# Adding gate sums and causal mask to attention scores: products on TensorE, or VectorE on PSUM

## The reference, cut to what matters

```python
log_f = jax.nn.log_sigmoid(f_logit).transpose(0, 2, 1)       # head x token
cum = jnp.cumsum(log_f, axis=-1)
for blk in range(n_blocks):                                  # 2 blocks of 128 queries
    logits = jnp.einsum('bhqd,bhkd->bhqk', qb, kb).astype(jnp.float32) * scale
    logits = logits + cum[:, :, start:end, None] - cum[:, :, None, :end]
    mask = jnp.arange(end)[None, :] <= (start + jnp.arange(Q_BLOCK))[:, None]
    logits = jnp.where(mask, logits, -jnp.inf)
    p = jax.nn.softmax(logits, axis=-1)
    outs.append(jnp.einsum('bhqk,bhkd->bhqd', p.astype(v.dtype), vb))
```

## Time and profile before

| What | Value |
|---|---|
| median of three runs | 3310.09 us |
| profiled execution, first to last instruction (span) | 3309.2 us |
| PE busy | 3296.3 us, 100% |
| PE weight loads busy | 2762.8 us, 83% |
| DVE busy | 2270.2 us, 69% |
| ACT busy | 1578.3 us, 48% |
| POOL busy | 731.1 us, 22% |
| DMA, mean | 243 GB/s |

### The profile page before, as it was taken

One profiled execution on the slowest core, in us unless ns is written; L12 is line 12 of the kernel. 1 busy time (PEld: TensorE's weight loads), 2 busy tenths in 40 slices (PEclk: granted clock), 3 DMA queues, 4 the chain that ended last, 5 costly groups with the idle time before them and its releaser, 6 DMA issues.

```text
span 3309.2 us, 42798 instructions
## 1 busy us (share of the span) xinstructions
PE 3296.3 (100%) x15846; PEld 2762.8 (83%) x15846; DVE 2270.2 (69%) x2218; ACT 1578.3 (48%) x1289; POOL 731.1 (22%) x559
## 2 busy tenths in 40 slices
PE   9999999999999999999999999999999999999999
PEld 7888888888888888878888888888888888888887
DVE  6675545698888788866577497444444777777778
ACT  7344344443333333354465345777777433333433
POOL 0000002400000000121000188888883000000000
PEclk9999999999999999999999999999999999999999
DMA  7555556888888888867555556777777666666663
GB/s 280 192 193 192 186 194 235 314 310 334 320 311 318 315 305 314 306 246 293 215 191 202 181 206 216 216 212 214 208 216 242 235 236 246 246 232 239 243 234 133
DMA packets 159559, 803.95 MB, mean 243 GB/s; under 512 B 51668, under 2 KB 52484, under 8 KB 70496
## 3 DMA queue, kind: packets, MB, share of 16 engines
q1 hardware_dynamic: 85728, 610.05, 50.2%
q0 software_dynamic: 67248, 170.03, 16.2%
q10 hardware_dynamic: 6480, 22.44, 1.8%
HBM read 759.23 MB, written 43.18 MB: 242 GB/s over the span
## 4 chain that ended last, share of the span: by engine, by line
PE 97%; ACT 1%; DMA 1%; DVE 0%; issue 0%; POOL 0%; SPq 0%; ACTq 0%
PE ps L2243 24%; PE ps L2245 24%; PE ps L2244 24%; PE ps L2763 12%; PE ps L2772 6%; PE ps L2283 1%; PE ps L2320 1%; PE ps L2322 1%; PE ps L2321 1%; DMA raw<-in_w_first 1%; PE ps L2431 0%; PE ps L2411 0%; ACT hi L648 0%; PE ps L2820 0%; PE ps L2419 0%
## 5 line engine op out<-in xcount | busy, mean ns | idle before, releaser
L648 ACT CAST hi<-raw 128x2048 fp32r<-128x2048 f32 x571 | 1090.9, 1912 | 1526.6 <-PE ps L2245 1354.8
L1279 DVE TENSOR_TENSOR lo<-raw,hi 128x2048 fp32r<-128x2048 f32 x436 | 997.6, 2290 | 364.6 <-ACT hi L648 349.0
L2243 PE MATMUL ps<-hi,hT 128*128 128x512 f32 x2064 | 816.0, 395 | 0.0
L2245 PE MATMUL ps<-hi,hT 128*128 128x512 f32 x2064 | 804.4, 390 | 0.0
L2244 PE MATMUL ps<-lo,hT 128*128 128x512 f32 x2064 | 803.9, 389 | 0.0
L2243 PEld LDWEIGHTS ps<-hi,hT 128*128 128x128 f32 x2064 | 387.7, 188 | 82.3 <-issue 4.8
L2245 PEld LDWEIGHTS ps<-hi,hT 128*128 128x128 f32 x2064 | 387.5, 188 | 82.1
L2244 PEld LDWEIGHTS ps<-lo,hT 128*128 128x128 f32 x2064 | 387.9, 188 | 77.6
L588 POOL DMA_INDIRECT w_scratch<-picks,cell x256 | 397.7, 1553 | 86.3 <-issue 83.8
L2763 PE MATMUL ps<-hT,hi 128*128 128x512 f32 x1728 | 412.2, 391 | 0.0
L2243 PE MATMUL ps<-hi,pactTh 128*128 128x512 f32 x992 | 386.6, 390 | 0.0
(11 more groups left out here) (424 smaller groups left out, 3111.2 us busy)
## 6 DMA issues: line engine op xcount, KB each, us to landing
raw<-in_w_peer SPq DMA_DIRECT2D x256, 1024.0 KB, 5.0
raw<-in_w_ffn SPq DMA_DIRECT2D x132, 1024.0 KB, 5.9
adaraw<-in_w_ada POOLq DMA_DIRECT2D x96, 1024.0 KB, 5.2
raw<-in_w_first SPq DMA_DIRECT2D x86, 1024.0 KB, 4.9
raw<-in_w_second SPq DMA_DIRECT2D x72, 1024.0 KB, 4.9
raw<-in_w_merge SPq DMA_DIRECT2D x28, 1024.0 KB, 6.0
w_scratch<-zeros POOLq DMA_DIRECT2D x16, 1024.0 KB, 11.8
wc<-w_scratch POOLq DMA_DIRECT2D x32, 512.0 KB, 4.8
```

The lines of the kernel that those rows point to most:

```text
L648: nc.scalar.copy(hi[:, s, :], raw[:, s, :]).then_inc(hi_done, 1)
L1279: V.tensor_tensor(lo[:, s, :], raw[:, s, :], hi[:, s, :].bitcast(F32), ALU.subtract).then_inc(lo_done, 1)
L2243: T.matmul(out, th[stat], hi[:, s, cut], start=start, stop=False)
L2245: return T.matmul(out, tl[stat], hi[:, s, cut], start=False, stop=stop)
```

## The change: what it does

The products with `gates` and with the causal mask are gone, and so are `lsums`, `gates`, the rounded identity and mask. The sums go once to DRAM (`cum_d`, with their negatives), and come back in two forms: `cumrow`, for each head its negative sums as a row on all 128 partitions, and `cumq`, for each head the sum at the query as a column. POOL adds the mask to a copy of the first half of the rows (`cumdiag`) and to the second half in place. DVE then adds column and rows to the scores in PSUM, one instruction for each block of queries, before it takes the maxima.

```diff
-            nc.gpsimd.memset(gates[:].bitcast(F32), 0.0).then_inc(sem("sel_in"), 1)
+            nc.gpsimd.memset(zeros[:], 0.0).then_inc(sem("sel_in"), 1)
             pool.wait_ge(sem("sel_in"), 2)
-            nc.gpsimd.memset(gates[0:4].bitcast(F32), 1.0).then_inc(sem("sel_in"), 1)
-            nc.gpsimd.memset(zeros[:], 0.0).then_inc(sem("sel_in"), 1)
...
             clear_weights(0, 6)
-            pool.wait_ge(sem("cum"), 2)
-            load_sums(0)
-            clear_weights(6, 13)
-            pool.wait_ge(sem("scores2"), 4)
-            load_sums(1)
-            clear_weights(13, 16)
+            pool.wait_ge(sem("cum"), 1)
+            pool.dma_start(cum_d, lgate[:, 1:3, :]).then_inc(sem("cum_in"), 16)
+            pool.wait_ge(sem("cum_in"), 16)
+            pool.dma_start(cumrow[:], bass.AP(cum_d.tensor, SEQ, [[0, P], [2 * SEQ, H2], [1, SEQ]])).then_inc(sem("cum_in"), 16)
+            with nc.allow_non_contiguous_dma(reason="a column of sums for each head"):
+                for k in range(TOK):
+                    pool.dma_start(cumq[:, k], bass.AP(cum_d.tensor, P * k, [[1, P], [2 * SEQ, H2]])).then_inc(sem("cum_in"), 16)
+            pool.wait_ge(sem("cum_in"), 64)
+            later = causal[:].rearrange("p (o n) -> p o n", o=1).to_broadcast([P, H2, P])
+            nc.gpsimd.tensor_tensor(cumdiag[:], cumrow[:, :, 0:P], later, ALU.add).then_inc(sem("sel_in"), 1)
+            nc.gpsimd.tensor_tensor(cumrow[:, :, P:SEQ], cumrow[:, :, P:SEQ], later, ALU.add).then_inc(sem("sel_in"), 1)
+            clear_weights(6, 16)
...
-                S = [lsums[:, r, :] for r in range(4)]
-                step(V.tensor_copy(S[0], L[1]))
-                step(V.tensor_tensor(S[1], L[1], S[0].bitcast(F32), ALU.subtract))
-                V.tensor_scalar(S[2], S[0].bitcast(F32), -1.0, None, ALU.mult).then_inc(sem("cum"), 1)
-                V.tensor_scalar(S[3], S[1].bitcast(F32), -1.0, None, ALU.mult).then_inc(sem("cum"), 1)
+                V.tensor_scalar(L[2], L[1], -1.0, None, ALU.mult).then_inc(sem("cum"), 1)
...
                         dve.wait_ge(sem("scores2"), h + 1)
+                        dve.wait_ge(sem("sel_in"), 4)
+                        for k, sums in enumerate((cumdiag, cumrow)):
+                            part = ps[:, 6, SEQ * k:SEQ * k + P * (k + 1)]
+                            ins = V.scalar_tensor_tensor(part, part, cumq[:, k, h:h + 1], sums[:, h], ALU.add, ALU.add)
+                        step(ins)
...
-                        V.tensor_copy(identr[:], ident[:]).then_inc(sem("wfl"), 1)
-                        V.tensor_copy(causalr[:], causal[:]).then_inc(sem("wfl"), 1)
...
-                    pe.wait_ge(sem("pair_in"), 64)
-                    pe.wait_ge(sem("wfl"), 3)
...
-                    T.matmul(out, qkT2[:, h, P * m:P * m + P], qkT2[:, 8 + h, 0:keys], start=True, stop=False)
-                    T.matmul(out, gates[:, 0, h % 4, P * m:P * m + P], gates[:, 1, h % 4, 0:keys], start=False, stop=False)
-                    ins = T.matmul(ps[:, 6, SEQ * m + P * m:SEQ * m + keys], identr[:], causalr[:], start=False, stop=True)
+                    ins = T.matmul(out, qkT2[:, h, P * m:P * m + P], qkT2[:, 8 + h, 0:keys], start=True, stop=True)
```

More of the change, by code:

```diff
@@ L144 @@
     "gy_T": "ACT: gelu of the turned gates", "qk_T": "DVE: turned queries and keys out of PSUM",
-    "wf_in": "DMA: forget weights", "wfh": "ACT: their leading part", "wfl": "DVE: and rest; then identity and causal mask rounded", "f_mm": "PE: forget logits",
+    "wf_in": "DMA: forget weights", "wfh": "ACT: their leading part", "wfl": "DVE: and rest", "f_mm": "PE: forget logits",
     "lg_abs": "DVE: logits' size, then -|lambda|", "lg_exp": "ACT: their exponentials", "cum": "DVE: sums of log gates",
-    "sel_in": "Pool: zeros around the forget weights, zeros, then ones around the log gates' sums, a row of zeros", "pair_in": "DMA: sums of four heads as rows", "scores2": "PE: heads' scores", "max2": "DVE: maxima",
+    "sel_in": "Pool: zeros around the forget weights, a row of zeros, log gates' sums with the causal mask",
+    "cum_in": "DMA: log gates' sums in DRAM, then as rows and as columns", "scores2": "PE: heads' scores", "max2": "DVE: maxima",
     "exp2": "ACT: exponentials (two a head)", "turned2": "PE: turned probabilities", "probs2": "DVE: these out of PSUM",
@@ L247, in program @@
     bx = at("bx", [P, 8, SEQ], F32, XO + 8 * K)
-    gates = at("gates", [P, 2, 4, SEQ], F32R, XO)
+    cumrow = at("cumrow", [P, H2, SEQ], F32, XO)
+    cumdiag = at("cumdiag", [P, H2, P], F32, XO + 8 * K)
     probs2 = at("probs2", [P, 2, TOK, SEQ], F32, A + 41 * K)
@@ L255, in program @@
     lgate = at("lgate", [8, 4, SEQ], F32, A + 49 * K)
-    lsums = at("lsums", [8, 4, SEQ], F32R, A + 49 * K)
     ga1 = at("ga1", [P, D], F32, A + 24 * K)
@@ L276, in program @@
     cell = at("cell", [P, TOK, 8, TOPK], U32, A + 51 * K)
-    zeros = at("zeros", [P, 2048], F32, XO + 8 * K)
+    zeros = at("zeros", [P, 1024], F32, XO + 12 * K)
     y = at("y", [P, TOK, D], F32, A)
@@ L295, in program @@
     causal = at("causal", [P, P], F32, CO + 4 * K)
-    identr = at("identr", [P, P], F32R, CO + 3 * K)
-    causalr = at("causalr", [P, P], F32R, CO + 3 * K + 512)
     small_at = [CO + 5 * K + 512]
@@ L324, in program @@
     row0 = at("row0", [P, 1], F32, CO + 4 * K + 256)
+    cumq = cmb[:].rearrange("p e k g -> p (e k g)")[:, 0:TOK * H2].rearrange("p (k h) -> p k h", h=H2)
     ps = nc.alloc_psum_tensor("ps", [P, 8, 512], F32)
@@ L358, in program @@
     w_d = nc.dram_tensor("w_scratch", [EXPERTS, SEQ], F32, kind="Internal").ap()
+    cum_d = nc.dram_tensor("sums_scratch", [H2, 2, SEQ], F32, kind="Internal").ap()
     hid_d = nc.dram_tensor("hidden_scratch", [EARLY - 1, P, TOK * 512], F32, kind="Internal").ap()
@@ L540, in _ @@
             pool.wait_ge(sem("x_moved"), 32)
-            nc.gpsimd.memset(gates[:].bitcast(F32), 0.0).then_inc(sem("sel_in"), 1)
+            nc.gpsimd.memset(zeros[:], 0.0).then_inc(sem("sel_in"), 1)
             pool.wait_ge(sem("sel_in"), 2)
-            nc.gpsimd.memset(gates[0:4].bitcast(F32), 1.0).then_inc(sem("sel_in"), 1)
-            pool.wait_ge(sem("sel_in"), 3)
-            nc.gpsimd.memset(zeros[:], 0.0).then_inc(sem("sel_in"), 1)
-            pool.wait_ge(sem("sel_in"), 4)
             def clear_weights(first, last):
@@ L551, in clear_weights @@
                     part = w_d[1024 * i:1024 * i + 1024].rearrange("(r a) t -> r (a t)", a=8)
[L552 to L556, removed]
+                    row = zeros[:].rearrange("p (o n) -> p o n", o=1).to_broadcast([P, 2, 1024])
+                    pool.dma_start(part.rearrange("r (o n) -> r o n", o=2), row).then_inc(sem("w_zero"), 16)
             clear_weights(0, 6)
-            pool.wait_ge(sem("cum"), 2)
-            load_sums(0)
-            clear_weights(6, 13)
-            pool.wait_ge(sem("scores2"), 4)
-            load_sums(1)
-            clear_weights(13, 16)
+            pool.wait_ge(sem("cum"), 1)
[10 more added lines that the diff above has]
+            clear_weights(6, 16)
             pool.wait_ge(sem("values2"), H2)
@@ L2631, in scores2 @@
                     pe.wait_ge(sem("qk_T"), 4)
-                    pe.wait_ge(sem("pair_in"), 128)
                 for m in range(TOK):
```

## The result

Five runs of the changed kernel took 3322.64 to 3324.12 us, median 3323.07; the kernel before, beside them, 3309.64 to 3311.64, median 3310.09. The ratio is 1.0039, 95% interval 1.0028 to 1.0049: slower by 13.0 us, and clear of noise. The forecast was 3319.8, the range 3312.5 to 3326.0. The profiled run was the longest of the five, 3324.12, with a span of 3322.5 us.

The account below looks back on a forecast made before the run. PE, busy for 112.81 of 113.00 us in the second attention, was taken as the bound. Head 0's late sums 6.0, clock 2.0 and heads 1 to 7 1.65 made +9.7: 3319.8 us, range 3312.5 to 3326.

Parts of the forecast that it names:

- dearer sums: Rival: at head 0 columns take 10.3, weight pieces and rows sharing engines; +9.7 there, 3323.5 us in all; chance 0.14.
- PE bounds, and its idle time is not taken back: Second attention: PE busy 112.81 of 113.00 us, so any wait moves the end by as much.
- g = 0.44 a head: PE's scores: four products of 0.11 us go at each head, 3.5 us for eight if PE never waited.
- d = 0.77 a head: DVE ahead of the maxima: two additions on PSUM and a wait add 0.77 us, bounds 0.52 and 1.00.
- d - 0.33 net where the pattern is bare: Heads 1, 4, 5 and 6: the turning starts 0.44 us later each, +1.76 together.
- Head 0: +6.0: Head 0's turning: sums return late through DRAM and POOL, so PE turns at 1540.0 instead of 1533.99.
- lands, with 6.6, at 1532.7: Sums' return for head 0: last columns issued at 1526.1 land after 6.6 us; bounds 1529.0 and 1536.4.
- The clock: +2.0, 0 to 3: Behind head 0's 6.2 us of PE idleness the clock falls to half and costs 2.0 us.
- The rival of prompt sums: Columns land after 2.9, head 0 costs +2.3, PE idles 2.5 us, clock holds: +4.0, 3314.1 us; chance 0.20.
- What costs nothing: DVE's dropped casts and small instructions, POOL's dropped fills, and ten clearing DMAs now behind the additions: no cost.

Follow-up runs that it names:

- e6: Changed kernel with sums fetched early from an input tensor, and DVE's additions and maxima moved ahead of the next `lo`: 3306.90 us.
- e2: Changed kernel with rows and columns fetched from an input tensor before the first clearing, so not the gate's sums: 3311.85 us.
- e3: Changed kernel without the two DMAs of columns; DVE adds 0.0 in the same instruction: 3320.21 us.
- e4: Changed kernel with the rows fetched early from an input tensor and only the columns late: 3318.47 us.
- e5: Changed kernel with a partition's rows laid out in DRAM as one run of 8 KB instead of eight of 1 KB: 3321.24 us.
- e9: The changed kernel run once more, unedited, beside e10: 3322.36 us.
- e11: Changed kernel with no columns and a partition's rows as one run of 8 KB: 3317.79 us.
- e10: e1 run once more, beside the changed kernel: 3323.33 us.
- e12: e2 with a third addition on 128x256 a head on DVE ahead of the maxima: 3315.77 us.
- e1: Changed kernel with 38 products of ones by ones put on PE ahead of head 0's turning, to fill its idle time: 3322.05 us.

## Why the prediction was right

It forecast a slowdown of 9.7 us; 13.0 came, inside the range. Each link of its path is in the trace, but the time came out 0.4 us below that of its rival "dearer sums", and the range held because it was drawn wide enough for that case. By its own steps:

1. *PE bounds, and its idle time is not taken back.* Right: behind the turning of head 7 the two traces run on 13.0 to 13.3 apart to the end.
2. *g = 0.44 a head.* Right in size: 0.46 to 0.48 in e6. That it would not be gained was right too (e2), and that it would be there once DVE's way is shorter was shown by e6.
3. *d = 0.77 a head, d - 0.33 net where the pattern is bare.* d was 0.78. The net was 0.47, 0.31 and 0.30 at heads 4, 5 and 6 for a forecast of 0.44; head 3 had 0.73 for 0.77, heads 2 and 7 -0.58 and -0.52 for -0.44. All in all heads 2 to 7 cost 0.71 where my terms give 1.21. A part is how it is read: a load that had waited starts with its product, one in the flow 0.2 ahead of it. The rest is not accounted for.
4. *Head 0: +6.0.* The mechanism was right, the size was off: 9.46 less 0.28, so 9.2. The step that failed is "lands, with 6.6, at 1532.7". The last columns landed at about 1536.2, after 10.3. I had counted the megabyte of rows ahead of them with its 0.9 of issue and no time of its own; e3, e4 and e5 show that it is the rows. That was the rival "dearer sums", forecast at 3323.5 with 0.14; its reason, weight pieces and rows that share the engines, is shown for the rows and argued for the pieces. The other links were near: DRAM 1.8 for 2.5, POOL 2.33 for 2.40 each, POOL's end to the turning 2.5 for 2.43.
5. *The clock: +2.0, 0 to 3.* Right in size: 2.6 in the changed kernel's trace, 1.4 in that of e9. It fell about 4.5 us after the last product's end at 1534.19 (0.87 is the mean of the window from 1538), at the program's end 4.9. In e3, e4, e5 and e11 it was 4.7 to 5.2, but in e9 2.1. So 4.9 was no bound to lean on. The rival of prompt sums took it for granted that the clock holds through 2.5 us of idleness; it fell behind 2.3 us in e10 and behind 1.9 in e12.
6. *What costs nothing.* Right: in this stretch no wait of PE for `lo`, for a weight piece or for the clearings shows in the changed kernel's trace.

Sum with the measured terms: 9.2 + 0.3 + 2.6 + 0.3 (head 1) + 0.7 = 13.1, against 13.3 between the spans.

## What to carry to other kernels

Work taken from the bounding engine is worth nothing where another engine's way between the same two events is longer (e2); measure the slack of the hand-over before counting it, and put what is added at a place where the other engine stands idle (e6). A chain of DMAs, each waited for, is priced link by link, each with its bytes as they land: the rows were 8 KB in DRAM but a megabyte on 128 partitions, and took 9.9 us. A stop of the matrix engine can cost more than its length: behind 9.3 us without products the half clock took 1.4 or 2.6 us more.

## What the runs showed that was not expected

- In e10 the clock fell 1.3 us *after* PE had gone back to work, behind about 2.3 us of idleness. In e1, with the same program and 2.0 us of idleness, it held.
- In e12 it fell at about the time at which PE went on, behind 1.9 us of idleness; some 1.6 us were lost by it.
- The same code lost 1.4 or 2.6 us to the clock in two runs, and the fall came 2.1 or 4.5 us after PE's last product.
- Filling PE's hole went with a longer chain of DMAs, by 1.2 and 1.4 us in two pairs of runs; why stays open.
